# Output projection to feed-forward in a two-layer block: the first 128 tokens are turned and multiplied ahead of the second 128

## The reference, cut to what matters

```python
for i in range(2):
    ...
    o = jnp.einsum('bse,ed->bsd', merge_heads(o), w_o[i])
    x = x + gt_a[:, None, :] * rmsnorm(o, g_mix_post[i])

    h = modulate(rmsnorm(x, g_ffn_pre[i]), sh_f, sc_f)
    gate = jnp.einsum('bsd,df->bsf', h, w_ffn_gate[i])
    up = jnp.einsum('bsd,df->bsf', h, w_ffn_up[i])
    gate = causal_depthwise_conv(gate, w_conv[i], b_conv[i])
    y = jnp.einsum('bsf,fd->bsd', jax.nn.silu(gate) * up, w_ffn_down[i])
    x = x + gt_f[:, None, :] * rmsnorm(y, g_ffn_post[i])
```

## Time and profile before

| what | us |
|---|---|
| median of 3 runs | 1478.21 |
| lowest, highest run | 1474.15, 1479.27 |
| the profiled execution | 1475.2 |
| its span, first to last instruction | 1473.2 |
| TensorE busy in the span | 1418.5 (96%) |
| granted clock of TensorE, mean | 0.994 |

### The profile page before, as it was taken

How to read it: one execution, slowest core, us unless ns; L and a number is a source line. 1 busy time by engine, 2 the same in 40 slices (tenths; PEclk the granted TensorE clock), 3 DMA queues, 4 the chain that set the end, 5 groups by cost and what they waited for, 6 DMA issues and landing times.

```text
span 1473.2 us, 23782 instructions
## 1 busy us (share of the span) xinstructions
PE 1418.5 (96%) x9502; PEld 938.2 (64%) x9503; DVE 632.0 (43%) x1121; ACT 227.1 (15%) x465; POOL 213.0 (14%) x150
## 2 busy tenths in 40 slices
PE   7999999999999999998999999999999999999997
PEld 5766755545445554444585649998448664999943
DVE  1545545221222212121553434557665472555666
ACT  1320003100000000000312531001031052200101
POOL 2000100000000000000000027770000002677100
PEclk9999899999999999999999999999999999999999
DMA  9954297999999999999999055345429923352610
GB/s 357 323 222 173 103 409 289 377 409 419 424 425 427 423 426 424 423 426 423 406 411 369 23 197 204 116 169 203 171 97 352 380 85 114 107 180 93 231 48 29
DMA packets 95186, 400.92 MB, mean 272 GB/s; under 512 B 7392, under 2 KB 12640, under 8 KB 67968
## 3 DMA queue, kind: packets, MB, share of 16 engines
q1 hardware_dynamic: 95104, 399.73, 68.8%
HBM read 398.66 MB, written 1.05 MB: 271 GB/s over the span
## 4 chain that ended last, share of the span: by engine, by line
PE 82%; DMA 11%; DVE 5%; issue 1%; ACT 1%; SPq 0%; POOL 0%; DVEq 0%; ACTq 0%
PE psum L1489 17%; PE psum L1146 15%; PE psum L1301 8%; PE psum L1541 8%; DMA ring<-in_moe_gate 5%; PE psum L1451 4%; PE psum L1132 3%; PE psum L711 3%; DMA arena<-in_moe_up 2%; DMA ring<-in_moe_up 2%; PE psum L1319 2%; PE psum L1521 2%; PE psum L1334 2%; PE psum L633 1%; DMA ring<-in_w_mod 1%; PE psum L753 1%
## 5 line engine op out<-in xcount | busy, mean ns | idle before, releaser
L1146 PE MATMUL psum<-ring,arena 128*64 128x256 f32 (+1 forms) x1728 | 235.4, 427 | 11.8 <-DMA ring<-in_moe_up 7.2
L1146 PEld LDWEIGHTS psum<-ring,arena 128*64 128x64 f32 x1728 | 125.8, 138 | 126.3 <-issue 74.2
L1489 PE MATMUL psum<-arena,ring 128*128 128x128 f32 x1280 | 150.4, 275 | 2.1 <-ACT arena L2325 2.0
L1489 PEld LDWEIGHTS psum<-arena,ring 128*128 128x128 f32 x1280 | 146.4, 192 | 2.8 <-issue 2.8
L1146 PE MATMUL psum<-arena 128*64 128x256 f32 (+1 forms) x812 | 109.6, 423 | 4.6 <-DMA arena<-in_moe_up 3.3
L1489 PE MATMUL psum<-arena 128*128 128x128 f32 x960 | 113.8, 275 | 0.0
L1301 PE MATMUL psum<-arena,ring 128*128 128x256 f32 x512 | 112.2, 380 | 1.5 <-DVE arena L1600 1.5
L584 POOL TENSOR_TENSOR arena<-ring 128x1024 f32<-128x1024 f32 x20 | 47.1, 2353 | 456.7 <-PE psum L1451 236.9
L1489 PEld LDWEIGHTS psum<-arena 128*128 128x128 f32 x960 | 110.4, 192 | 0.0
L1964 DVE TENSOR_TENSOR arena<-psum,arena 128x256 f32<-128x256 f32 x32 | 13.6, 425 | 223.6 <-PE psum L1146 223.6
L1301 PEld LDWEIGHTS psum<-arena,ring 128*128 128x128 f32 x512 | 96.8, 190 | 16.6 <-issue 3.6
(11 more groups left out here) (436 smaller groups left out, 1775.1 us busy)
## 6 DMA issues: line engine op xcount, KB each, us to landing
ring<-in_moe_up SPq DMA_DIRECT2D x22, 2048.0 KB, 24.2
ring<-in_moe_down SPq DMA_DIRECT2D x22, 2048.0 KB, 23.7
ring<-in_moe_gate SPq DMA_DIRECT2D x21, 2048.0 KB, 24.1
arena<-in_w_mod SPq DMA_DIRECT2D x32, 1024.0 KB, 8.0
ring<-in_ada_w SPq DMA_DIRECT2D x12, 2048.0 KB, 10.5
ring<-in_w_qkv SPq DMA_DIRECT2D x12, 2048.0 KB, 14.1
arena<-in_moe_gate SPq DMA_DIRECT2D x20, 1024.0 KB, 23.5
arena<-in_moe_down SPq DMA_DIRECT2D x20, 1024.0 KB, 22.1
```

Of the source, the lines that this page charges most:

```text
L1146: ins = mm(bank[b][o, 0:n], lhsT, w[:, half * n:(half + 1) * n], start=first, stop=last, tile_position=(0, 64 * half))
L1489: last = mm(bank[b + k][:, slot * P:slot * P + P], left[:, k, c], right[:, c, :], start=(c == 0), stop=(c == 3))
```

## The change

**TensorE's order.** The eight transposes of the first tokens (`turn_half(0)`) and the gain rows now stand between the sums (1,0) and (1,1). After (1,1), and in layer 0 after `fill1(2)`, come w11 and w12 of pair 0 for the first tokens (`first_lower(0)`, `first_upper(0)`) and in layer 1 also w12 of pair 1 (`first_upper(1)`). Then the second tokens are turned (`turn_half(1)`), and s4 of pair 0 follows. The idle products of this passage are gone.

**Waits.** `half_ready(t, 8)` waits for all eight chunks of a half at once. `flush` stands behind s4 now. `evac_half` moves chunks of 128 columns: four for each half on VectorE and four on ScalarE, so 16 instructions a layer in place of 8. `turned` is told after the sixth and the eighth transpose of a half.

**Banks.** The sums of the projection go to banks 2 to 5. A half is turned into the two banks of its own sums: 2 and 3 for t = 0, 4 and 5 for t = 1. Pairs use (2,3) and (6,7) or (4,5) and (0,1). The squares are written to `QT`, since `hTd` is in use earlier.

```diff
+                def turn_half(t):
+
+                    pe.wait_ge(S("xn_ready"), 2 * (h_n - 1) + t)
+                    if t == 0:
+                        pe.wait_ge(S("x3_ready"), 2 * layer + 1)
+                    for c in range(DC):
+                        if t == 1 and c == 4:
+                            pe.wait_ge(S("xn_ready_s"), h_n)
+                        last = nc.tensor.transpose(half_turned(t, c), yt[:, t, c * P:(c + 1) * P], ident[:, :])
+                        if c in (5, 7):
+                            last.then_inc(S("turned"), 1)
+
                 for t in range(NT):
                     for n in range(2):
+                        if (t, n) == (1, 1):
+                            turn_half(0)
+                            rows(diagd, 4 + 2 * layer, 6, ("rows_copied", 6 + 4 * layer))
                         for c in range(DC):
-                            last = mm(bank[1 + 2 * t + n][:, :], oT[:, c, t * P:(t + 1) * P], w[n][:, c, :],
+                            last = mm(bank[2 + 2 * t + n][:, :], oT[:, c, t * P:(t + 1) * P], w[n][:, c, :],
                                       start=(c == 0), stop=(c == DC - 1))
...
                 if layer == 0:
                     fill1(2)
-                rows(diagd, 4 + 2 * layer, 6, ("rows_copied", 6 + 4 * layer))
-                h_n = turn_again(2 + 2 * layer, (((5, 0), (5, 0)), ((5, 1), (5, 2)))[layer])
...
+                pair_loaded(0)
+                half_ready(0, 8)
+                first_lower(0)
+                pe.wait_ge(S("rows_copied"), 8 + 4 * layer)
+                first_upper(0)
+                if layer == 1:
+                    pe.wait_ge(S("mod_copied"), 10)
+                    first_upper(1)
+                turn_half(1)
+                half_ready(1, 8)
...
+                    if p > 0:
+                        first_lower(p)
+                    if p == 1 and layer == 0:
+                        pe.wait_ge(S("mod_copied"), 8)
+                    if p > layer:
+                        first_upper(p)
+                    pe.wait_ge(S("wsum_ready"), FAST * layer + p + 1)
+                    product(s4, hi[:, :, P:TOK], x0, 1)
                     if p == 0 and layer == 0:
                         flush()
-                    pe.wait_ge(S("wsum_ready"), FAST * layer + p + 1)
-                    product(s4, hi[:, :, P:TOK], x0, 1)
                     if p == 0:
                         pe.wait_ge(S("pair_ready"), 67 * layer + 1)
                     product(s2, hsum[:, 1], y0, 1)
...
                 scaled_first(5 + 4 * layer)
+                evac_half(0, lm, 12 + 8 * layer)
                 weighted(1, 1, 8 * layer, gmixb)
                 residual(1, 4 * layer, "x3_ready")
                 scaled_second(6 + 4 * layer)
-                evac_h(hTd, lm, 24, 12 + 8 * layer)
+                evac_half(1, lm, 12 + 8 * layer)
...
+            def evac_half(t, lm, n, fc):
+
+                act.wait_ge(S("fcol_ready"), fc)
+                for c in (2, 3, 6, 7):
+                    act.wait_ge(S("turned"), n + 2 * t + 2)
+                    a_.to(A(hTd[:, c, t * P:t * P + P], half_turned(t, c), ACT.Identity,
+                            bias=modc[:, lm, 24 + c:25 + c], scale=fcol[:, c:c + 1]), "h_ready_s")
...
                 y_half(1, 0, 8 * layer + 3, True)
+                evac_half(0, lm, 12 + 8 * layer, 4 + 2 * layer)
+                row_copies(gffnb, 4 + 2 * layer, 6)
                 y_half(1, 1, 8 * layer + 4, False)
                 row_norm(1, yt, "x3_ready", 2 * layer + 2)
                 scaled_rest()
-                evac_h(hTd, lm, 24, 12 + 8 * layer, 4 + 2 * layer)
-                row_copies(gffnb, 4 + 2 * layer, 6)
```

More of the change, by code:

```diff
@@ L1459, in _, with product, half_ready, pair_loaded @@
                     fill1(2)
-                rows(diagd, 4 + 2 * layer, 6, ("rows_copied", 6 + 4 * layer))
-                h_n = turn_again(2 + 2 * layer, (((5, 0), (5, 0)), ((5, 1), (5, 2)))[layer])
                 n0 = st_pe.n
                 F0 = NFT * layer
-                def up_pair(p):
-                    n = n0 + 2 * (p // 2)
[L1470 to L1477, removed]
+                lo, hi = hTd[:, 0:4], hTd[:, 4:8]
+                def product(left, right, b, slot, freed=None):
+                    for k in range(2):
+                        for c in range(4):
+                            last = mm(bank[b[k]][:, slot * P:slot * P + P], left[:, k, c], right[:, c, :],
+                                      start=(c == 0), stop=(c == 3))
+                            if freed == k and c == 0:
+                                last.then_inc(S("slot_freed"), 1)
+                    return last
+                def half_ready(t, chunks):
+                    for name in ("h_ready_v", "h_ready_s"):
+                        pe.wait_ge(S(name), H_BEFORE[h_n] + 4 * t + chunks // 2)
+                def pair_loaded(p):
+                    n = n0 + 2 * (p // 2)
                     if p % 2 == 0:
@@ L1480, in up_pair @@
                             pe.wait_ge(S(f"slot{(n + k) % RING}_loaded"), 16 * ((n + k) // RING + 1))
[L1482 to L1493, removed]
@@ L1495, in up_pair, with first_lower, first_upper @@
-                    lo, hi = hTd[:, 0:4], hTd[:, 4:8]
-                    product(w11, lo[:, :, 0:P], y0, 0, 0 if p % 2 == 0 else None)
-                    product(w12, hi[:, :, 0:P], x0, 0)
+                def first_lower(p):
+                    product(pair_weights(n0, p)[0], lo[:, :, 0:P], pair_banks[p % 2][0], 0, 0 if p % 2 == 0 else None)
+                def first_upper(p):
+                    product(pair_weights(n0, p)[1], hi[:, :, 0:P], pair_banks[p % 2][1], 0)
+                pair_loaded(0)
@@ new lines, in _, with up_pair @@
+                half_ready(0, 8)
[7 more added lines that the diff above has]
+                half_ready(1, 8)
+                def up_pair(p):
+                    w11, w12, w21, w22 = pair_weights(n0, p)
+                    s1, s2, s4 = (wsum[p % 2][:, i] for i in range(3))
+                    y0, x0 = pair_banks[p % 2]
+                    if p >= 2:
+                        pe.wait_ge(S("act_f"), F0 + 2 * p - 2)
+                        pair_loaded(p)
+                    if p > 0:
[6 more added lines that the diff above has]
+                    product(s4, hi[:, :, P:TOK], x0, 1)
@@ L1601, in evac_h, with evac_half @@
                                     modc[:, lm, sh0 + c:sh0 + c + 1], ALU.mult, ALU.add), "h_ready_v")
+            def evac_half(t, lm, n):
+                for c in (0, 1, 4, 5):
+                    dve.wait_ge(S("turned"), n + 2 * t + 1)
+                    d.to(V.tensor_scalar(hTd[:, c, t * P:t * P + P], half_turned(t, c), fcol[:, c:c + 1], modc[:, lm, 24 + c:25 + c], ALU.mult, ALU.add), "h_ready_v")
             d.to(V.memset(part, 0.0), "part_zeroed")
@@ L2499, in row_norm, with y_half @@
                 a_.to(A(stat[:, 2 + t:3 + t], stat[:, t:t + 1], ACT.Exp, scale=-0.5), "rstd_ready")
-            def y_half(t, n, done, first):
+            def y_half(t, n, done, first, squared=QT, b0=2):
                 act.wait_ge(S("sum_done"), done)
                 u = 2 * t + n
-                a_.to(A(hTd[:, 2 * u:2 * u + 2, :], bank[1 + u].rearrange("p (c t) -> p c t", c=2), ACT.Square,
+                a_.to(A(squared[:, 2 * u:2 * u + 2, :], bank[b0 + u].rearrange("p (c t) -> p c t", c=2), ACT.Square,
                         scale=D ** -0.5, accum_out=half_sq[:, u:u + 1]), "sq_done")
@@ L2630, in _ @@
                 for k, (t, n) in enumerate(((0, 1), (1, 0), (0, 0), (1, 1))):
-                    y_half(t, n, 8 * layer + 4 + k + 1, k < 2)
+                    y_half(t, n, 8 * layer + 4 + k + 1, k < 2, hTd, 1)
                 if layer == 0:
```

29 lines of the change are left out of this document (20 added, 9 removed).

## The result

| | before | after |
|---|---|---|
| median of 22 runs each, us | 1476.68 | 1483.62 |
| lowest, highest, us | 1470.8, 1480.67 | 1478.79, 1489.08 |
| the profiled execution, us | 1475.2 | 1482.58 |
| its span | 1473.2 | 1480.6 |
| TensorE busy in the span | 1418.5 | 1415.9 |

A forecast was written before the change was run, and what follows sets the result against it. TensorE, with 82% of the chain, was taken to bound the kernel. New waits less removed idle time gave +6.7 us, clock falls +2.6; these 9.3 on the median of 1478.21 made 1487.5 us, range 1480 to 1492.

The forecast's parts named there:

- First wait: TensorE ahead of the first tokens' transposes and (1,1), waiting for VectorE's scaled_first: 2.53 us in layer 0, 2.54 in layer 1.
- Second wait: TensorE ahead of s4 of pair 0, waiting for all chunks of the second tokens: 2.38 us in each layer.
- hsum: TensorE after s4 of pair 0, waiting for VectorE's token_sums: 0.32 us in layer 0, 1.13 us in layer 1.
- GpSimd: TensorE at s4 of pair 1, waiting for GpSimd's sums: 0.87 us in layer 1, nothing in layer 0.
- The sum at an unchanged clock: Both passages with all waits, less the idle time removed: +3.8 us in layer 0, +2.9 in layer 1, together +6.7.
- What was costed at nothing: Second slot_freed and one weight load some 5 us later per layer, and everything from pair 2 on: no cost.
- The clock: Granted clock falls to half behind two of the four long waits, mean price 1.3 us each: +2.6, bounds 0 and 5.2.
- The base: The median of the kernel before, 1478.21 us, to which the forecast added its 9.3 us.
- (a): Rival: the waits come without a fall of the clock, +6.7 us, 1484.9 us; chance 0.28.
- (b): Rival: the clock falls behind all four waits or stays down longer, +12 or more, 1490 us and above; chance 0.08.
- (c): Rival: the overlap works without new waits and wins the 5.5 us of removed waits, 1472.7 us; chance 0.04.
- (d): Rival: waits mostly shorter than forecast, about +3 to +4 us, 1481.5 us, no measurable change; chance 0.16.

The follow-up runs named there:

- b_busy: The changed kernel with matmuls without use filling the first and second waits on TensorE in both layers; 1479.77 us against 1475.43 before, ratio 1.0051.
- a_inside: The changed kernel with the first tokens' transposes and gain rows after four of the eight matmuls of (1,1); 1478.51 us against 1475.43 before, ratio 1.0033.
- g_scaled: The changed kernel with scaled_first ahead of weighted(1,0) in VectorE's list, both layers; 1478.16 us against 1475.43 before, ratio 1.0024.
- e_both: The changed kernel with first transposes inside (1,1), gain rows behind it, second tokens turned ahead of products; 1473.04 us against 1476.52 before, ratio 0.9986; repeated, 0.9978.
- after_look: The changed kernel, unaltered, profiled once more for the clock in a second trace; 1486.35 us.
- c_order: The changed kernel with gain rows behind (1,1) and the second tokens turned ahead of products, first wait left; 1479.38 us against 1475.43 before, ratio 1.0032.

## Why the prediction was right, and where its numbers were off

The forecast was slower, 1487.5 us in a range of 1480 to 1492; the median is 1483.62, and the loss 7.1 us where 9.3 was forecast. The 9.3 lies just above the interval of the loss, 5.2 to 9.0 us, and the 6.7 without the clock lies inside it: the direction and the waits are confirmed, the term of the clock in whole runs is not.

- **First wait: right.** From the end of (1,0) to the first transposes 2.55 us in both layers, where 2.53 and 2.54 were forecast. Two edits take it away in different ways: against b_busy, a_inside wins 2.64 and 2.65 us in the two layers, g_scaled 2.09 and 2.57.
- **Second wait: right, 0.1 us too long.** Four chunks of 128 columns took 1.93 us on ScalarE, as worked out from the other line's 367 and 473 ns. s4 started 3.24 us after its transposes in layer 1 (1265.58 to 1268.82), where 3.34 was forecast, and 3.19 us in layer 0.
- **hsum: right.** The bracket of b_busy says 0.91 us in layer 1, but it counts from the drained end of s4, while the forecast counts from start to start: from s4 to s2 it had 1.79 + 1.13 = 2.92 us, and 1263.79 to 1266.72 is 2.93. In layer 0 the gap behind flush is 0.26 us (890.13 + 0.81 to 891.20) for 0.32.
- **GpSimd: right.** The bracket says 0.61 us; from s2 of pair 0 to s4 of pair 1 the forecast had 7.16 + 1.79 + 0.87 = 9.82 us, and 1266.72 to 1276.53 is 9.81. In layer 0 there is no wait.
- **The sum at an unchanged clock: right.** +3.8 and +2.9 were forecast; b_busy measured +3.78 and +2.79.
- **What was costed at nothing: right.** From pair 2 of layer 1 on the kernel takes 190.0 to 190.1 us in all eleven traces, and from pair 1 of layer 0 to the end of (1,0) of layer 1 it takes 347.9 to 348.0 us in all but the three named above, so the later slot_freed and the later weight load do not show.
- **The clock: the mechanism right, the size not settled.** In the profiled execution two of four waits were followed by a fall, as forecast, at a price of 1.7 (forecast 1.7) and 0.0 us (forecast near 0.4); in the second one it was three. That is 1.7 and 3.3 us for a term of 2.6. That the count of two came true in the first trace is luck in part, since the second has three. The 1.4 us for a fall behind the second wait of layer 0 was never met: none came there in four traces. The loss of the medians less the waits, 7.1 - 6.6 = 0.5 us, is under that term, with an interval of 2 us either way. The mean clocks of whole runs do point to more falls: 0.994 over after's 22 runs, 0.996 over the 69 runs of before beside the experiments, 0.997 over b_busy's 12. What those falls cost in whole runs stays open. A fall ahead of later waits is swallowed by them, as in layer 1 here.
- **The base.** The median of before over 22 runs is 1.5 us under the one of three runs to which the sum was added. With the median of 22 runs as base the forecast would have been 1486.0. Of the remaining 2.4 us the waits account for 0.1 (6.7 forecast, 6.57 measured); the rest stands against the clock's term and is about as large as what the measurement leaves open.

Of the rivals, (a) has the nearest time, 1484.9, nearer than the forecast itself (1483.4 on the median of 22 runs), but not the mechanism: falls were there in both traces of after, and none of its 22 runs was above a mean clock of 0.996, where 29 of the 69 runs of before were. (b), a fall behind all four, did not occur in either trace. (c), the overlap as named, would have needed scaled_first earlier and a cover over the chunks; e_both covered both waits and won 3.0 of the 5.5 us. (d) is excluded by the interval of whole runs only narrowly, 5.2 us where it gave +3 to +4, and clearly by the stretches, 6.57 us at an unchanged clock. Of the fourteen waits of 2.4 to 2.5 and of 2.15 us in the traces of after, after_look, c_order, a_inside and g_scaled, eight were followed by a fall, so by the runs it is a risk and not a certainty.

## What to carry to other kernels

When a stage is split in two so that the first half starts early, look at where the first half's input is made ready relative to the instruction that now waits for it, and put as much ready work of the old stage in front of it as the wait is long: here four of eight matmul steps turned a wait of 2.5 us into none. Do the same at the far end, where the second half's chunks need something to lie under: turning the second half ahead of one product was worth 1.7 us in layer 1, and ahead of two 2.6 us in layer 0 (e_both against a_inside). On VectorE, an instruction whose input has long been there should not stand behind one that waits for the newest sum.

## What the runs showed of the hardware

VectorE and GpSimd slow each other far more than expected when both add from SBUF: VectorE's 128x512 sum went from 0.69 to 2.71 us and GpSimd's 128x1024 sum from 2.35 to 2.67 us, over three sums in each layer. Each of VectorE's sums ended 0.54 to 0.55 us after one of GpSimd's, so VectorE finished one sum for each of GpSimd's. The Trainium skill (GPSIMD Engine Reference, 1. Specifications) says that GpSimd shares its SBUF interfaces with VectorE, with contention for instructions with two SBUF inputs; the traces agree.

The granted clock fell to 0.50 behind waits of 2.15 us too (after, 1270 to 1273 us). Behind the first wait of layer 1 of one and the same kernel it fell in one execution (after_look) and not in the other (after): waits repeat to 0.01 us from one execution to the next, falls of the clock need not. A single trace of this kernel is therefore good for the waits and not for the clock.
